# Banded attention of a streaming encoder layer: each split float32r product triple against one plain float32 product

## Chip, cores and metric

The kernel runs on one core of a Trainium2 chip. The metric is device microseconds (us) from start to end. TensorE (PE) multiplies, VectorE (DVE), ScalarE (ACT) and GpSimd (POOL) do the rest, and DMA queues move data between HBM and SBUF. A difference of about 0.2% (3.3 us) is the least that a measurement of this kernel tells from no change.

## What is computed

One layer of a chunk-causal streaming encoder on 1024 prompt tokens and 64 sample tokens, in float32. The part in question is the banded attention of the mixer: 8 heads of 64, chunks of 64 tokens, each chunk attending to itself and the 8 chunks before it.

```python
def chunk_band_attention(qc, kb, vb, key_valid, rel_bias, offset):
    ...
    s = jnp.einsum('bnqhd,bnkhd->bnhqk', qc, kb).astype(jnp.float32) * (HEAD_DIM_B ** -0.5) + bias[None, None]
    s = jnp.where(key_valid[None, :, None, None, :], s, NEG)
    p = jax.nn.softmax(s, axis=-1).astype(vb.dtype)
    return jnp.einsum('bnhqk,bnkhd->bnqhd', p, vb)
```

Before it come an input projection, two convolution mixers and the RMS norms of q and k; after it an output projection, cross attention and an MLP.

## The kernel before

Activations lie transposed, features on the partitions and 1092 token columns along the free axis. The large projections run through `pe_part` (L444), which multiplies a value split into a high and a low float32r part as high·high + high·low + low·high. The banded attention is written in the same way.

It is done for four head pairs j = 0..3, one after another, and each pair in nine units b = 0..8 of 128 queries (36 units n = 9j + b). Unit b has min(b+1, 5) key blocks of 128 (the last one, the sample tokens, reads 512 cached keys and 64 new ones). The two heads of a pair lie on partitions 0 to 63 and 64 to 127.

A unit passes through these steps:

- `scores(n)` on PE (L2397): for each head, three products q_hi·k_hi, q_lo·k_hi, q_hi·k_lo into PSUM banks 0 to 2.
- `biased(n)` on DVE (L1804): adds the bias tile of the pair and takes the row minimum, once per head. It waits for `bias_ready`, two memsets on POOL (L895, L897) that follow the DMA of the bias tile.
- `exps(n)` on ACT (L1229): exponential with the row sum, in place in `scores`.
- `transposes(n)` on PE (L2461): 128x128 transposes of the exponentials, up to ten, into banks 4 to 6, in up to three pieces of two key blocks.
- `pt_hi(n)` on ACT (L1247) copies each piece to float32r, and `pt_lo(n)` on DVE (L1827) forms the rest.
- `values(n)` on PE (L2483): three products per key block, 128x256, into bank 7; `o_out(n)` on ACT (L1238) copies the result out.

PE runs the cycle of unit n in program order: `transposes(n)`, an item a, `values(n-1)`, `scores(n+2)`, an item b. The items are small jobs for the next head pair: x = 0..2 and 3..5 broadcast the RMS factors of q and k through PE (L2390) for a multiplication on DVE (L1764), x = 6..8 transpose the v columns (L2383) for a copy, and x = 9..11 divide the output by the sums. After the first pair all items use PSUM bank 3, so PE starts an item only when the consumer of the last one has read that bank. DVE runs the cycle as the piece copies of unit n, item a, `biased(n+2)`, item b. Each engine takes its instructions strictly in this written order.

For pair 0 the nine items and the high and low parts of q, k and v are made before `scores(0)`. For the later pairs ACT makes the high parts (`q_hi`, `k_hi`, `v_hi`, `cache_hi`), DVE the low part of v and POOL those of q, k and the cache (L423, L429).

Of the kernel before, what the change touches and what calls it, by code (L numbers as in the profile page):

```python
# [13 lines left out]
P = 128  # L14
# [36 lines left out]
class Semaphores:  # L51

    def __init__(self, sem):
# [78 lines left out]
        self.qk2_hi = sem("qk2_hi")  # L132
        self.qk2_lo = sem("qk2_lo")
        self.kc_hi = sem("kc_hi")
        self.kc_lo = sem("kc_lo")
        self.v_hi = sem("v_hi")
        self.v_lo = sem("v_lo")
# [7 lines left out]
        self.pt_hi = sem("pt_hi")  # L145
        self.pt_lo = sem("pt_lo")
# [73 lines left out]
class BandOperands:  # L220

    def __init__(self, Q, K, V, KC, VC):
        self.Q, self.K, self.V, self.KC, self.VC = Q, K, V, KC, VC

# [5 lines left out]
def build(nc, xT, memT, slabs, wdn, params, rbrev, ctxa, ctxc, kcT, vc, mkcT, mvc,  # L230
          o_y, o_ca, o_cc, o_k, o_v, o_kc, o_vc, o_mk, o_mv):
    ctx = ExitStack()
    with ctx:
# [55 lines left out]
        QKV = [slot(f"q_raw{j}", 12 + j) for j in range(4)] + [slot(f"k_raw{j}", 8 + j) for j in range(4)] \  # L289
# [5 lines left out]
        for r in range(2):  # L295
            o = A0 + 8 * r * TB
            AT.append(BandOperands(
                Q=[at(f"q_hi{r}", [P, T], F32R, o), at(f"q_lo{r}", [P, T], F32R, o + TB)],
                K=[at(f"k_hi{r}", [P, T], F32R, o + 2 * TB), at(f"k_lo{r}", [P, T], F32R, o + 3 * TB)],
                V=[at(f"v_hi{r}", [P, 9, P], F32R, o + 4 * TB), at(f"v_lo{r}", [P, 9, P], F32R, o + 4 * TB + 4608)],  # L300
                KC=[at(f"kc_hi{r}", [P, 512], F32R, o + 4 * TB + 9216),
                    at(f"kc_lo{r}", [P, 512], F32R, o + 4 * TB + 11264)],
                VC=[at(f"vc_hi{r}", [P, 4, P], F32R, o + 4 * TB + 13312),
                    at(f"vc_lo{r}", [P, 4, P], F32R, o + 4 * TB + 15360)]))
# [3 lines left out]
        PT = [[at(f"pt_{n}{r}", [P, 4, 256], F32R, W0 + 4096 * (2 * r + x)) for x, n in enumerate(("hi", "lo"))]  # L308
              for r in range(2)]
        PT5 = [[at("pt5_hi0", [P, 256], F32R, W0 + 16384), at("pt5_lo0", [P, 256], F32R, W0 + 17408)],  # L310
               [at("pt5_hi1", [P, 256], F32R, W0 + 23552), at("pt5_lo1", [P, 256], F32R, B0 + 15360)]]
# [4 lines left out]
        RKC = at("kc_raw", [P, 512], F32, R0 + 4608)  # L316
        RVC = at("vc_raw", [P, 4, P], F32, R0 + 6656)
# [98 lines left out]

        def cache_lo(e, j):

            r = AT[j % 2]
# [127 lines left out]
        for n in range(N_U):  # L547
            CUM.append(CUM[-1] + pieces(n))

# [2250 lines left out]
```

## Time and profile before

| | |
|---|---|
| median of 3 runs | 1665.53 us (1664.52 to 1666.72) |
| profiled execution | 1665.04 us |
| its span (first to last instruction) | 1663.3 us |
| mean granted TensorE clock | 0.981 of full speed |
| PE / DVE / ACT / POOL busy | 95% / 59% / 40% / 18% |
| chain that ended last | PE 82%, DVE 5%, ACT 4%, DMA 4%, issue 3% |

The span and the profiled execution's time differ by 1.7 us of start and end around the instructions. The chain is the sequence of work that ended last, followed back through what each step waited for. A mean over the program hides that the attention stage has other limits than the projections around it, so that stage has to be read alone.

### The profile page before, as it was taken

The numbers are of one execution on the slowest core, as the hardware profiler recorded it, in microseconds if no ns is written. First come the engines' busy times: TensorE is split into PE (matmuls) and PEld (weight loads), VectorE is DVE, ScalarE is ACT, GpSimd is POOL, SyncE is SP. The second block draws the span as 40 slices with busy tenths as digits, with TensorE's granted clock in tenths as the row PEclk, the third lists the DMA queues.
The fourth block names the chain that finished last, engine by engine and source line by source line (L and its number), as shares of the span: only waits on it lengthen the run. The fifth ranks groups of instructions, "written<-read, shape, count | busy, mean of one in ns | idle before, by whom it ended". The sixth has DMA issues, their size and how long they took to land.

```text
span 1663.3 us, 27523 instructions
## 1 busy us (share of the span) xinstructions
PE 1580.0 (95%) x11220; PEld 1545.5 (93%) x11220; DVE 980.6 (59%) x1393; ACT 658.1 (40%) x1154; POOL 305.3 (18%) x354
## 2 busy tenths in 40 slices
PE   6999999997889999997789999999999899999999
PEld 6999999995788899997679999999999899999999
DVE  6626776536778644245653477666666558646653
ACT  5521021136889532124531363333333333333332
POOL 1011000002220010002410005444455411010110
PEclk9999999988999999999989999999999999999999
DMA  7425111002110153101051215333333686354563
GB/s 245 143 91 171 40 39 39 26 1 93 37 37 34 51 174 134 48 14 51 26 184 54 92 40 184 146 146 145 146 145 147 234 288 220 96 168 147 159 211 110
DMA packets 63666, 189.37 MB, mean 114 GB/s; under 512 B 7872, under 2 KB 13048, under 8 KB 63408
## 3 DMA queue, kind: packets, MB, share of 16 engines
q1 hardware_dynamic: 37904, 91.11, 16.6%
q0 software_dynamic: 25648, 96.65, 16.1%
q8 instruction: 83, 1.36, 0.3%
q14 instruction: 31, 0.25, 0.1%
HBM read 138.58 MB, written 54.12 MB: 116 GB/s over the span
## 4 chain that ended last, share of the span: by engine, by line
PE 82%; DVE 5%; ACT 4%; DMA 4%; issue 3%; POOL 1%; SPq 0%; ACTq 0%; DVEq 0%; POOLq 0%
PE ps L454 33%; PE ps L2707 18%; PE ps L2728 17%; PE ps L2235 3%; PE ps L483 2%; PE ps L2483 2%; DMA a<-wdn 2%; PE ps L2606 2%; PE ps L2423 1%; PE ps L2461 1%; DVE scores L1804 1%; ACT scores L1229 1%; DVE t_raw L2084 1%; PE ps L505 1%; PE ps L2390 1%
## 5 line engine op out<-in xcount | busy, mean ns | idle before, releaser
L454 PE MATMUL ps<-A_hi,w_hi 128*128 128x364 f32 x768 | 173.6, 335 | 0.0
L454 PE MATMUL ps<-A_hi,w_lo 128*128 128x364 f32 x768 | 170.0, 329 | 0.0
L454 PE MATMUL ps<-A_lo,w_hi 128*128 128x364 f32 x768 | 169.9, 329 | 0.0
L395 DVE TENSOR_TENSOR w_lo<-w_raw,w_hi 128x1024 fp32r<-128x1024 f32 x43 | 52.5, 1223 | 151.6 <-ACT w_hi L391 151.2
L391 ACT ACTIVATE w_hi<-w_raw 128x1024 fp32r<-128x1024 f32 x42 | 44.3, 1057 | 241.5 <-PE ps L454 136.3
L454 PEld LDWEIGHTS ps<-A_lo,w_hi 128*128 128x128 f32 x768 | 134.4, 189 | 0.0
L454 PEld LDWEIGHTS ps<-A_hi,w_lo 128*128 128x128 f32 x768 | 134.0, 189 | 0.0
L454 PEld LDWEIGHTS ps<-A_hi,w_hi 128*128 128x128 f32 x768 | 133.7, 190 | 0.0
L2707 PE MATMUL ps<-t_hi,wq_hi 128*128 128x272 f32 x480 | 100.9, 292 | 7.2 <-DVE hid_stage L2130 4.3
L2707 PE MATMUL ps<-t_lo,wq_hi 128*128 128x272 f32 x480 | 100.5, 291 | 0.0
L2707 PE MATMUL ps<-t_hi,wq_lo 128*128 128x272 f32 x480 | 100.1, 290 | 0.0
L2728 PE MATMUL ps<-r_hi_a,wq_hi 128*128 128x272 f32 x448 | 93.3, 290 | 3.1 <-DVE r_lo_a L2170 3.1
L2728 PE MATMUL ps<-r_lo_b,wq_hi 128*128 128x272 f32 x448 | 93.5, 290 | 0.0
L2728 PE MATMUL ps<-r_hi_b,wq_lo 128*128 128x272 f32 x448 | 93.3, 289 | 0.0
L2728 PE MATMUL ps<-r_hi_b,wq_hi 128*128 128x272 f32 x448 | 93.3, 289 | 0.0
L2728 PE MATMUL ps<-r_lo_a,wq_hi 128*128 128x272 f32 x448 | 93.1, 289 | 0.0
L2728 PE MATMUL ps<-r_hi_a,wq_lo 128*128 128x272 f32 x448 | 93.0, 289 | 0.0
L2707 PEld LDWEIGHTS ps<-t_hi,wq_hi 128*128 128x128 f32 x480 | 76.3, 191 | 7.8 <-issue 7.8
L2707 PEld LDWEIGHTS ps<-t_lo,wq_hi 128*128 128x128 f32 x480 | 76.7, 192 | 0.0
L2707 PEld LDWEIGHTS ps<-t_hi,wq_lo 128*128 128x128 f32 x480 | 76.4, 191 | 0.0
L1655 DVE SCALAR_TENSOR_TENSOR conv_acc<-ua_ext,params,conv_acc 128x1118 f32<-128x1118 f32 x58 | 76.1, 1375 | 0.0
L2707 PE MATMUL ps<-A_hi,wq_lo 128*128 128x272 f32 x360 | 74.5, 288 | 0.0
(342 smaller groups left out, 4095.1 us busy)
## 6 DMA issues: line engine op xcount, KB each, us to landing
w_raw<-slabs SPq DMA_DIRECT2D x68, 512.0 KB, 3.4
quads_d<-quad_sum POOLq DMA_DIRECT2D x64, 272.0 KB, 3.2
w_raw<-wdn POOLq DMA_DIRECT2D x32, 512.0 KB, 4.1
r_raw_a<-quads_d SPq DMA_DIRECT2D x56, 272.0 KB, 2.9
r_raw_b<-quads_d SPq DMA_DIRECT2D x56, 272.0 KB, 2.9
quads_d<-hid_stage POOLq DMA_DIRECT2D x48, 272.0 KB, 2.8
Y<-xT POOLq DMA_DIRECT2D x16, 546.0 KB, 4.7
y_d<-Y POOLq DMA_DIRECT2D x16, 546.0 KB, 3.1
```

What stands on the lines that cost most here:

```text
L391: e.activation(WH[:, par], RAW[:, par], ACT.Copy).then_inc(s.w_hi, 1)
L395: e.tensor_tensor(WL[:, par], RAW[:, par], WH[:, par].bitcast(F32), ALU.subtract).then_inc(s.w_lo, 1)
L454: ins = e.matmul(PS[:, 3 * par + c, 0:CH], wt[:, wpar, w], xt[:, col:col + CH], start=(first and n == 0 and m == 0), stop=(last and n == l ...
L483: ins = e.matmul(PS[:, 6, 2 * b:2 * b + 2], src[:, t0:t0 + P], rhs[:, :], start=(n == 0), stop=(n == len(pairs) - 1))
L505: ins = e.transpose(PS[:, bank, BLK[b] - lo:BLK[b] - lo + P], src(b), ID[:, :])
L1229: e.activation(SS[n % 2][:, h, 0:cols], SS[n % 2][:, h, 0:cols], ACT.Exp, bias=MIN[:, m:m + 1], scale=-1.0, accum_out=ESUM[:, n, h:h + 1]) ...
L1655: e.scalar_tensor_tensor(CAV[:, h], UE[:, h, j:j + CAW], w, CAV[:, h], ALU.mult, ALU.add)\
L2235: ins = e.matmul(PS[:, 3 * par, 0:NMEM], wt[:, par, k * P:(k + 1) * P], xt[:, k * NMEM:(k + 1) * NMEM], start=(k == 0 and m == 0), stop=(k ...
L2483: ins = e.matmul(PS[:, 7, 0:256], lhs, rhs, start=(kt == 0 and m == 0), stop=(kt == tiles - 1 and m == 2))
L2606: ins = e.matmul(PS[:, 6 + d, 0:w], r.KV[vx][:, vv, v0:v0 + P], XPT[px][:, k, 0:w], start=(n == 0), stop=(n == 5))
L2707: ins = e.matmul(PS[:, b + c, 0:HC], WQ[wx][:, q % 4, k * P:(k + 1) * P], right(i, xx, k, c), start=(i in (0, 1, 3) and k == 0 and m == 0) ...
L2728: ins = e.matmul(PS[:, 2 * g + c, 0:HC], WQ[wx][:, down_slot(n), g * P:(g + 1) * P], down_right(xx, n)[:, c * HC:(c + 1) * HC], start=(ii ...
```

## The change

Each split product of the banded attention becomes one product of plain float32 operands. The high and low parts, and all instructions that made them, are gone: `q_hi`, `k_hi`, `cache_hi`, `v_hi` on ACT, `qk_lo` and `cache_lo` on DVE and POOL. `scores` reads `q_raw` and `k_raw` directly, with the order of its parts changed, and waits for q and k in thirds and not for the whole. The cache goes by DMA straight into its operand tiles. The v blocks are copied once, on DVE (`v_copy`). Of the transposed exponentials ACT copies piece 0 and DVE pieces 1 and 2, each once (`pt_copy`). For pair 0 the items run in the order 0, 3, 1, 2, 4 to 8, with `scores(0)` and `biased(0)` after the second of them and `scores(1)` and `biased(1)` after the fourth. The q and k tiles of the pairs lie in other slots.

```diff
-            def pt_hi(n):
-                for p in range(pieces(n)):
-                    rows, w = piece(n, p)
-                    e.wait_ge(s.t_done, CUM[n] + p + 1)
-                    if n >= 2:
-                        e.wait_ge(s.pv_done, n - 1)
-                        e.wait_ge(s.pt_lo, CUM[n - 1])
-                    e.activation(pt_piece(0, n, p), PS[0:rows, 4 + p, 0:w], ACT.Copy).then_inc(s.pt_hi, 1)
+            def pt_copy(n):
+                rows, w = piece(n, 0)
+                e.wait_ge(s.t_done, CUM[n] + 1)
+                if n >= 2:
+                    e.wait_ge(s.pv_done, n - 1)
+                e.activation(pt_piece(n, 0), PS[0:rows, 4, 0:w], ACT.Copy).then_inc(s.pt_act, 1)
...
-            def pt_lo(n):
-                for p in range(pieces(n)):
+            def pt_copy(n):
+                for p in range(1, pieces(n)):
                     rows, w = piece(n, p)
-                    e.wait_ge(s.pt_hi, CUM[n] + p + 1)
-                    e.tensor_tensor(pt_piece(1, n, p), PS[0:rows, 4 + p, 0:w], pt_piece(0, n, p).bitcast(F32),
-                                    ALU.subtract).then_inc(s.pt_lo, 1)
+                    e.wait_ge(s.t_done, CUM[n] + p + 1)
+                    if n >= 2:
+                        e.wait_ge(s.pv_done, n - 1)
+                    e.tensor_copy(pt_piece(n, p), PS[0:rows, 4 + p, 0:w]).then_inc(s.pt_dve, 1)
...
-            for x in range(9):
+            e.wait_ge(s.ya_done, 2)
+            for n, x in enumerate(FIRST_ITEMS):
                 item(0, x)
-                if x in (5, 8):
-                    qk_lo(e, 0, (x - 5) // 3)
-            e.wait_ge(s.ya_done, 2)
-            biased(0)
-            biased(1)
+                if n in (1, 3):
+                    biased(n // 2)
...
                 if tail <= 0:
-                    for m in range(3):
-                        ins = [part(h, m, M[h]) for h in range(2)]
-                    ins[0].then_inc(s.s_done, 1)
-                    ins[1].then_inc(s.s_done, 1)
+                    for h in range(2):
+                        part(h, M[h]).then_inc(s.s_done, 1)
                     return
...
+                part(1, M[1])
                 if b == 8:
-                    for m in range(3):
-                        part(1, m, (r.K, SEQ, 64, 512))
-                e.wait_ge(s.s_done, 2 * n + 1)
-                for m in range(3):
-                    ins = part(1, m, X[1])
-                ins.then_inc(s.s_done, 1)
+                    part(1, (K, SEQ, 64, 512))
+                part(0, X[0]).then_inc(s.s_done, 1)
+                part(0, M[0]).then_inc(s.s_done, 1)
+                e.wait_ge(s.s_done, S_CUM[n] + 1)
+                part(1, X[1]).then_inc(s.s_done, 1)
...
-                    for m, (vx, px) in enumerate(((0, 0), (0, 1), (1, 0))):
-                        if b < 8:
-                            lhs = r.V[vx][:, max(0, b - 4) + kt]
-                        else:
-                            lhs = r.VC[vx][:, kt] if kt < 4 else r.V[vx][0:w, 8]
-                        rhs = PT[n % 2][px][0:w, kt] if kt < 4 else PT5[n % 2][px][0:w, :]
-                        ins = e.matmul(PS[:, 7, 0:256], lhs, rhs,
-                                       start=(kt == 0 and m == 0), stop=(kt == tiles - 1 and m == 2))
+                    if b < 8:
+                        lhs = r.V[:, max(0, b - 4) + kt]
+                    else:
+                        lhs = r.VC[:, kt] if kt < 4 else r.V[0:w, 8]
+                    rhs = PT[n % 2][0:w, kt] if kt < 4 else PT5[n % 2][0:w, :]
+                    ins = e.matmul(PS[:, 7, 0:256], lhs, rhs, start=(kt == 0), stop=(kt == tiles - 1))
```

On PE, the scores of a unit with five key blocks (128x512 is the main part of one head, 128x128 its tail) were these before:

```order
L2423 MATMUL ps<-k_hi_104,q_hi_102 128x128 [waits ttr_done]
L2423 MATMUL ps<-k_hi_104,q_hi_102 128x512
L2423 MATMUL ps<-k_hi_104,q_lo_103 128x128
L2423 MATMUL ps<-k_lo_105,q_hi_102 128x128
L2423 MATMUL ps<-k_hi_104,q_hi_102 128x512
L2423 MATMUL ps<-k_hi_104,q_lo_103 128x512 x2
L2423 MATMUL ps<-k_lo_105,q_hi_102 128x512 x2
L2423 MATMUL ps<-k_hi_104,q_hi_102 128x128 [waits s_done]
```

In the change the same place, with the values of the unit before it (L2400), reads:

```order
L2400 MATMUL ps<-pt_112,v_102 128x256 [waits pt_act,o_used]
L2400 MATMUL ps<-pt_112,v_102 128x256
L2400 MATMUL ps<-pt_112,v_102 128x256 [waits pt_dve]
L2400 MATMUL ps<-pt_112,v_102 128x256
L2400 MATMUL ps<-pt_114,v_102 128x256 [waits pt_dve]
L2347 MATMUL ps<-k_raw_89,q_raw_85 128x512 [waits ttr_done]
L2347 MATMUL ps<-k_raw_89,q_raw_85 128x128
L2347 MATMUL ps<-k_raw_89,q_raw_85 128x512
L2347 MATMUL ps<-k_raw_89,q_raw_85 128x128 [waits s_done]
```

Twelve score products became four, and fifteen value products five. The parts of the two heads alternated product by product; now each head's part stands as one instruction.

On DVE, at the start of pair 0, these rows stood before (neg_max rows belong to the bias step):

```order
L1764 SCALAR_TENSOR_TENSOR k_raw_89<-k_raw_89,params,ps 128x384 [waits bc_done] x2
L1764 SCALAR_TENSOR_TENSOR k_raw_89<-k_raw_89,params,ps 128x324 [waits bc_done]
L429 TENSOR_TENSOR q_lo_103<-q_raw_85,q_hi_102 128x1092 [waits qk2_hi]
L1772 TENSOR_TENSOR v_lo_107<-ps,v_hi_106 128x384 [waits v_hi] x2
L1772 TENSOR_TENSOR v_lo_107<-ps,v_hi_106 128x256 [waits v_hi]
L1775 TENSOR_TENSOR v_lo_107<-ps,v_hi_106 64x128
L429 TENSOR_TENSOR k_lo_105<-k_raw_89,k_hi_104 128x1092 [waits qk2_hi]
L1804 ISA scores_122,neg_max<-ps,bias_124 128x128 [waits s_done,bias_ready,ya_done]
```

And these stand there now:

```order
L1690 SCALAR_TENSOR_TENSOR q_raw_85<-q_raw_85,gq_scaled,ps 128x384 [waits bc_done,ya_done,gq_ready]
L1690 SCALAR_TENSOR_TENSOR k_raw_89<-k_raw_89,params,ps 128x384 [waits bc_done]
L1731 ISA scores_108,neg_max<-ps,bias_110 128x128 [waits s_done,bias_ready]
L1731 ISA neg_max 128x1
L1731 ISA scores_108,neg_max<-ps,bias_110 128x128
L1731 ISA neg_max 128x1
L1690 SCALAR_TENSOR_TENSOR q_raw_85<-q_raw_85,gq_scaled,ps 128x384 [waits bc_done]
L1690 SCALAR_TENSOR_TENSOR q_raw_85<-q_raw_85,gq_scaled,ps 128x324 [waits bc_done]
L1731 ISA scores_109,neg_max<-ps,bias_110 128x256 [waits s_done,bias_ready]
```

The first bias step, with its wait for `bias_ready`, moved ahead of seven of the nine items of pair 0.

## Rows read from the trace of the kernel before

**Rows 1.** Work by stage: us, then busy us (and count) of PE, weight loads, DVE, ACT, POOL, then granted clock, DMA share, GB/s.

```profile
385.00:560.00 175.00, 152.09 (x1215) 134.72 (x1214) 127.19 (x301) 147.29 (x357) 32.66 (x33) 0.95 0.13 45
```

**Rows 2.** Chain that ended last, in order of time: start us, length us, what.

```profile
461.40 1.09 PE ps L2461 x10
...
473.27 0.37 PE ps L2461 x2
...
514.26 0.37 PE ps L2461 x2
...
553.71 0.48 PE ps L2390 x3
...
560.19 1.90 PE ps L483 x18
```

**Rows 3.** PE's first transposes of each unit, timeline: start us, us, engine, line, operation, xcount.

```profile
392.45 0.69 PE L2461 MATMUL ps<-ident,scores 128*128 128x128 f32 x2
...
433.97 0.44 PE L2461 MATMUL ps<-ident,scores 128*128 128x128 f32 x2
...
439.67 0.82 PE L2461 MATMUL ps<-ident,scores 128*128 128x128 f32 x6
444.90 1.04 PE L2461 MATMUL ps<-ident,scores 128*128 128x128 f32 x8
450.01 1.26 PE L2461 MATMUL ps<-ident,scores 128*128 128x128 f32 x10
455.42 1.25 PE L2461 MATMUL ps<-ident,scores 128*128 128x128 f32 x10
461.24 1.25 PE L2461 MATMUL ps<-ident,scores 128*128 128x128 f32 x10
465.59 1.31 PE L2461 MATMUL ps<-ident,scores 128*128 128x128 f32 x10
```

**Rows 4.** Timeline of one cycle with two items: [idle before <-releaser] at the end.

```profile
452.47 0.28 PE L2483 MATMUL ps<-pt_lo,v_hi 128*128 128x256 f32 x1
...
453.61 0.28 PE L2483 MATMUL ps<-pt_hi,v_lo 128*128 128x256 f32 x1
453.81 0.50 PE L2423 MATMUL ps<-k_hi,q_hi 64*128 64x128 f32 x2
...
455.03 0.55 PE L2390 MATMUL ps<-ident,rstd_heads 128*128 128x128 f32 x3
455.26 0.82 DVE L1804 CUSTOM_DVE_ANT_0 scores<-ps,bias 128x640 f32<-128x640 f32 x1 [1.30 <-issue]
...
457.42 0.55 PE L2390 MATMUL ps<-ident,rstd_heads 128*128 128x128 f32 x3 [0.75 <-DVE k_raw L1764]
```

**Rows 5.** Timeline, scores of a unit with 512 keys: six products.

```profile
438.16 0.50 PE L2423 MATMUL ps<-k_hi,q_hi 64*128 64x512 f32 x2
...
438.73 0.39 PE L2423 MATMUL ps<-k_lo,q_hi 64*128 64x512 f32 x2
```

**Rows 6.** Plain float32 products (line 483): duration ns min/median/max, first and last start.

```profile
L483 PE MATMUL ps<-half_sel,square x144: 166/251/251, 235.2 to 338.8; 128*128 128x2 f32 x144
```

**Rows 7.** Groups of the stage 385 to 553: busy us, mean ns, idle before with its releasers.

```profile
L1827 DVE TENSOR_TENSOR pt_lo<-ps,pt_hi 128x512 fp32r<-128x512 f32 (+2 forms) x84 | 45.6, 589 | 6.2 <-ACT pt_hi L1247 5.6
L1247 ACT ACTIVATE pt_hi<-ps 128x512 fp32r<-128x512 f32 (+2 forms) x84 | 38.9, 526 | 8.1 <-PE ps L2461 7.5
```

**Rows 8.** Timeline at the start of pair 0, POOL and DVE.

```profile
379.95 1.81 DVE L1764 SCALAR_TENSOR_TENSOR q_raw<-q_raw,gq_scaled,ps 128x384 f32<-128x384 f32 x3
...
388.99 0.20 POOL L897 MEMSET bias<- 64x128 f32 x1
...
390.94 0.29 DVE L1804 CUSTOM_DVE_ANT_0 scores<-ps,bias 128x128 f32<-128x128 f32 x1 [1.23 <-PE ps L2423]
```

**Rows 9.** Work by stretch, columns as in rows 1.

```profile
394.00:398.00 4.00, 4.00 (x19) 2.64 (x17) 1.75 (x6) 3.61 (x12) 0.00 (x0) 0.50 0.00 0
...
482.00:486.00 4.00, 4.00 (x25) 3.59 (x25) 1.25 (x3) 2.55 (x8) 1.43 (x2) 0.60 0.00 0
```

More of the change, by code:

```diff
@@ L288, in build @@
         CAV = at("conv_acc", [P, 2, CAW], F32, B0 + 9216)
-        QKV = [slot(f"q_raw{j}", 12 + j) for j in range(4)] + [slot(f"k_raw{j}", 8 + j) for j in range(4)] \
+        QKV = [slot(f"q_raw{j}", (14, 8, 10, 12)[j]) for j in range(4)] \
+            + [slot(f"k_raw{j}", (15, 9, 11, 13)[j]) for j in range(4)] \
             + [slot(f"v_raw{j}", 7 - j) for j in range(4)]
@@ L297, in build @@
             AT.append(BandOperands(
[L298 to L304, printed above, removed]
+                V=at(f"v{r}", [P, 9, P], F32, o + 4 * TB),
+                KC=at(f"kc{r}", [P, 512], F32, o + 4 * TB + 9216),
+                VC=at(f"vc{r}", [P, 4, P], F32, o + 4 * TB + 13312)))
         SS = [at(f"scores{r}", [P, 2, 640], F32, B0 + 5120 * r) for r in range(2)]
         BIAS = [at("bias0", [P, 2, 640], F32, B0 + 10240), at("bias1", [P, 2, 640], F32, W0 + 18432)]
[L308 to L311, printed above, removed]
+        PT = [at(f"pt{r}", [P, 4, 256], F32, W0 + 5120 * r) for r in range(2)]
+        PT5 = [at(f"pt5{r}", [P, 256], F32, W0 + 5120 * r + 4096) for r in range(2)]
         RX = at("rstd_heads", [P, 9, 2, 64], F32, R0)
@@ L600, in score_cols @@
             return PS[:, 0:3].rearrange("p a b -> p (a b)")[:, c0:c0 + cols], c0
+        S_CUM = [0]
+        for n in range(N_U):
+            S_CUM.append(S_CUM[-1] + (3 if n % 9 >= 4 else 2))
         RXN = {(0, 0): 1, (0, 1): 2}
@@ L1268, in _ @@
             rstd_heads(0, 1)
-            q_hi(0)
-            k_hi(0)
-            for c in range(3):
-                v_hi(0, c)
             exps(0)
             for n in range(N_U):
-                pt_hi(n)
+                pt_copy(n)
                 if n + 1 < N_U:
@@ L1857, in ya_norm @@
                 ins.then_inc(s.bc_used, 1)
-            for x in range(9):
+            e.wait_ge(s.ya_done, 2)
+            for n, x in enumerate(FIRST_ITEMS):
                 item(0, x)
-                if x in (5, 8):
-                    qk_lo(e, 0, (x - 5) // 3)
-            e.wait_ge(s.ya_done, 2)
-            biased(0)
-            biased(1)
+                if n in (1, 3):
+                    biased(n // 2)
             for n in range(N_U):
@@ L2450, in transposes @@
                 for p in range(pieces(n)):
-                    if n:
-                        e.wait_ge(s.pt_lo, CUM[n - 1] + min(p + 1, pieces(n - 1)))
+                    if n and p == 0:
+                        e.wait_ge(s.pt_act, n)
+                    elif n and CUM_D[n]:
+                        e.wait_ge(s.pt_dve, CUM_D[n - 1] + min(p, pieces(n - 1) - 1))
                     if p == 2 and last[6]:
```

164 lines of the change are left out of this document (50 added, 114 removed).

## Prediction

> **What bounds the kernel now.** I read the clock first (0.981, one core, nothing to compare), then the work by stage. In the attention stage PE is busy for 152 of 175 us and ACT for 147 [rows 1]; the projections before and after it do not change. So the question is what the end of the attention does, when item (3,11) on PE (553.71, 0.48 us long [rows 2]) lets the first out-projection product start. Everything behind it waits for PE and should move as one block.
>
> The chain of waits runs from pair 0 to the middle of pair 3 mostly over PE's own instructions. The starts of the transposes give the period of each unit. In pair 1 they are 433.97, 439.67 (b = 2), 444.90, 450.01, 455.42, 461.24, 465.59 [rows 3], and 473.27 for the next pair [rows 2]. As periods: 5.70 for b = 0 and 1 together, then 5.23, 5.11, 5.41, 5.82, 4.35, and 7.68 for b = 7 and 8, which is 39.3 us for the pair. Pair 0 takes 41.5 (392.45 to 433.97 [rows 3]), pair 2 takes 41.0 (473.27 to 514.26), pair 3 takes 39.5 (514.26 to 553.71 [rows 2]).
>
> One cycle shows why. PE ends the scores at 455.03; DVE needs until 457.42 (two bias steps of about 0.82 and an item) before PE may start the next item, and PE stands idle for 0.75 of these 2.39 us [rows 4]. The rest is PE at work. So a pair is PE work plus about 4 us of such stalls, in cycles b = 2 to 5. ACT's and DVE's work counts only through those stalls and in pair 3, where ACT also squares and splits for the next stage.
>
> **The price of a plain product.** The trace has none with a wide moving operand, so I bound it. The statistic products of line 483 are plain float32 with 2 columns. The program has 8 times 9 of those with half_sel, and the trace shows x144 [rows 6]: a plain product is recorded as two passes. Eighteen records take 1.90 us [rows 2], 0.106 us each, for 2 columns: the floor of a pass. Ten float32 transposes take 1.09 us [rows 2], 0.109 each for 128 columns in one pass. So a pass costs at most about 0.107 per 128 columns, if a product streams as a transpose does. A float32r value product takes (453.61 - 452.47)/10 = 0.114 for 256 columns [rows 4].
>
> Low end: a plain pass streams as fast as float32r, 256 columns in 0.114, so a value product is 0.23. High end: 0.214 per pass, 0.43 per product. I take the high end: the operand is plain float32, and the row nearest in operand type is the transpose. At 0.43 one plain product costs more than the three split ones, 0.34.
>
> The Trainium skill (FP8 and Floating Point Precision, TensorE Precision Notes) says that true float32 takes four passes through the array. No run here shows it for a wide product. By it a value product would cost four times 0.107, the same 0.43.
>
> **Values.** 140 key blocks: 140 x 0.43 = 60 us against 140 x 0.34 = 48. That adds 12 us.
>
> **Scores.** The heads use different halves of the rows, and their products run side by side: two pairs of 512-column products start within 0.57 us (438.16 to 438.73 [rows 5]), 0.29 per pair where one alone streams for 0.21 to 0.23. Of a five-block unit the twelve products take 455.03 - 453.81 = 1.22 us [rows 4]. In the change a 512-column pass lasts 0.43, and each head's two passes follow each other. If the next head's first pass starts beside the last head's second, a five-block unit takes 7/2 of such passes, 1.5 us; if nothing overlaps, 5 x 0.43 = 2.13. For b = 0 to 3: 0.43, 0.64, 0.96, 1.28 with overlap and up to 0.43, 0.85, 1.28, 1.71 without. For b = 8: 1.6 to 2.2 against 1.3.
>
> **What is removed.** ACT loses 48 of 84 piece copies of 0.526, and DVE 36 of 84 of 0.589 [rows 7], besides all q, k, v and cache splits. In cycles b = 2 to 5 of pairs 0 to 2 this buys little: the stall there is the bias steps and the item, which stay. I let the stall end 2.0 us after the transposes start (2.39 less the item b of 0.33 on PE); for b = 2, whose v copy no longer goes ACT then DVE, 1.75.
>
> **New periods**, T for transposes at 0.107 each, item 0.33:
> - b = 0: T 0.2 + values 2.13 + scores 0.96 to 1.28 = 3.3 to 3.6. b = 1: 0.43 + 0.33 + 0.43 + 1.28 to 1.71 + 0.33 = 2.8 to 3.2. Together 6.1 to 6.8 against 5.70.
> - b = 2: 1.75 + 0.33 + values 0.85 + 1.5 to 2.13 + 0.33 = 4.8 to 5.4 against 5.23.
> - b = 3, 4, 5: 2.0 + 0.33 + values 1.28, 1.71, 2.13 + scores + 0.33 = 5.5, 5.9, 6.3 to 6.1, 6.5, 6.9 against 5.11, 5.41, 5.82.
> - b = 6: 1.07 + 2.13 + 1.6 to 2.2 = 4.8 to 5.4 against 4.35. b = 7 and 8: each T 1.07 + item 0.33 + values 2.13, and the scores 0.43 and 0.64 to 0.85 of the next pair's first units: 8.1 to 8.3 against 7.68.
>
> Sum 41.5 to 45.4 us: pair 1 gets 2.2 to 6.1 us longer, and pair 2, which before took 1.7 us more (at 482 to 486 PE was granted 0.60 of its clock [rows 9]), 0.5 to 4.4.
>
> **Pair 3.** No items b. ACT's extra squares hold b = 1 and 2 as before, less one copy: about 0.4 us back. The last units have no scores left. Period by period I get 37.6 to 40.5 against 39.5: -1.9 to +1.0.
>
> **The start of pair 0.** DVE does one q item of about 0.6 at 379.95 (three took 1.81 [rows 8]) and one k item behind it, so `scores(0)` can run at about 382. But the first bias step waits for the memset that ends at 389.19, only 1.75 us ahead of where it started before (390.94) [rows 8]; the DMA ahead of it keeps its place. DVE stands still from about 382, for some 7 us, and seven items are queued behind: the transposes of unit 0 come after item 8 on PE. From 389.2: bias 0.5, two items 1.2, a wait for scores(1) 0.4, bias 0.85, two items 1.2, first v copy and its wait 0.8, last v transposes 0.9: about 395.1 against 392.45, so +2.6. Hidden before, by work that DVE did while the bias tile was on its way. PE is nearly idle till then. It had the lower of its two levels, 0.50 (1.2 GHz), in 394 to 398 [rows 9], and will have it again, with passes twice as long in units 0 to 2: +0.6. From there pair 0 follows the periods above, less the wait for the cache DMA that ACT had: +0.5 to +3.7. Pair 0 in all: +3.7 to +6.9.
>
> **Sum.** 4.5 to 18.4 us: pair 0 3.7 to 6.9, pair 1 2.2 to 6.1, pair 2 0.5 to 4.4, pair 3 -1.9 to 1.0. I believe in overlap of the heads, since float32r shows it, so I stay in the lower half; small per-pass floors come on top. I take +10.5. The profiled execution is 1665.04 and the median 1665.53, so 1676.
>
> **Rivals.**
> - *No overlap between the heads' plain passes.* For it: each head's passes now stand together. Against it: rows 5. The high ends of all sums: +18, 1684. Chance 0.2.
> - *Fast plain passes* (the other side): 256 columns in 0.114. The place is every values and scores step: five-block units need 1.14 for values and 0.86 for scores (8 passes of 0.107), so periods b = 2 to 5 fall to 3.7 to 4.7 and the others to 2.3 to 3.6. A pair takes about 32.5, 7 us less in pairs 1 and 2; pairs 0 and 3 gain 8 together: -22, 1643. It decides once a 256-column product costs less than about 0.34. For it: no row excludes it, since transposes may be held by their weight loads. Against it: the operand type. Chance 0.09.
> - *Weight loads not hidden.* A plain pass would pay its stream and its load of 0.106 in turn. 280 value passes give +30 and the scores about +15 over my sum: 1720. Against it: float32r hides the load (256 columns in 0.114). The Trainium skill (TensorE: Matmul & The Clock Gate, Part 3) says that weight loads overlap running products only where the row group differs. By that rule both passes of a product would pay; the trace disagrees for float32r, and no row shows plain. Chance 0.05.
> - *The stalls shrink.* If DVE, relieved, lets items go 0.7 us earlier in twelve cycles, 8 us come back: about 1667, no change. Against it: bias steps and item alone fill the 2.39 us. Chance 0.11.
>
> **How the numbers follow.** My case (1671 to 1680) has 0.55. The range reaches to no overlap above and to the vanished stalls below: 1665 to 1688. A difference of 0.2% is about what a measurement tells. Slower: my case, no overlap and unhidden loads, 0.80, less 0.03 for a sum that lands near zero: 0.77. Same: the shrunk stalls and that 0.03, less a little: 0.12. Faster: 0.11.
>
> **What would show it.** PE's value records: two per product, starts 0.21 apart. Scores of a five-block unit: 1.5 us. Transposes of unit 0 at 395, those of pair 1 at 438 to 441; pair 1 some 42 to 44 us long; an idle DVE from 382 to 389; ACT busy far less with no gain. The prediction is wrong if value records start 0.11 apart, or if the idle PE time in cycles b = 2 to 5 disappears.

## The result, and the profile after

| | before | changed kernel |
|---|---|---|
| median | 1666.22 us (1660.99 to 1672.52, 16 runs) | 1669.99 us (1665.79 to 1679.33, 16 runs) |
| profiled execution, span | 1665.04, 1663.3 us | 1670.03, 1668.2 us |
| mean granted clock | 0.981 | 0.982 |

The ratio is 1.0033 with an interval of 1.002 to 1.0047: the change costs 3.3 to 7.8 us. The forecast was 1676 with a range of 1665 to 1688, and slower at 0.77. The direction and the range held. The size did less well: 1.0033 is 5.5 us, about half of the +10.5 that was taken.

The busy times of the whole program, on the page of the changed kernel, have moved as if the change were harmless: ACT falls from 40% to 37% and DVE from 59% to 58%, while PE goes from 95% to 96%.

```profile
PE 1595.2 (96%) x10964; PEld 1534.9 (92%) x10964; DVE 960.6 (58%) x1353; ACT 622.7 (37%) x1074; POOL 283.4 (17%) x342
...
PE 84%; DVE 5%; DMA 4%; ACT 3%; issue 3%; POOL 1%; SPq 0%; DVEq 0%; ACTq 0%; POOLq 0%
```

The chain of waits dates the pairs: the first transposes of pairs 1, 2 and 3, a five-block set of values, and item (3,11), the answers to [rows 2].

```profile
437.00 0.37 PE ps L2377 x2
...
467.92 2.16 PE ps L2400 x10
...
480.21 0.37 PE ps L2377 x2
...
523.42 0.37 PE ps L2377 x2
...
563.52 0.48 PE ps L2314 x3
```

Pair 1 lasts 480.21 - 437.00 = 43.2 us (39.3 before), pair 2 lasts 43.2 (41.0), pair 3 lasts 40.1 (39.5).

To compare executions I measure the stage from a mark at which both kernels have done the same work: from the start of DVE's last `v_raw` instruction of the projection to item (3,11). The two marks in front, before and after the change:

```profile
377.48 1.29 DVE L1594 TENSOR_TENSOR v_raw<-ps,rstd 128x1092 f32<-128x1092 f32 x1 [2.07 <-PE ps L454]
```

```profile
378.75 1.29 DVE L1520 TENSOR_TENSOR v_raw<-ps,rstd 128x1092 f32<-128x1092 f32 x1 [2.70 <-PE ps L428]
```

The stage was 553.71 - 377.48 = 176.2 us and is 563.52 - 378.75 = 184.8: 8.5 us more. The work between these marks, before and after (columns as in [rows 1]; the window of [rows 1] itself reaches 6 us into the next projection before the change and ends inside the stage after it):

```profile
377.48:553.71 176.23, 151.28 (x1216) 132.65 (x1216) 129.32 (x310) 147.71 (x357) 36.79 (x40) 0.95 0.14 47
```

```profile
378.75:563.52 184.77, 166.52 (x960) 121.73 (x960) 105.69 (x270) 112.14 (x276) 14.09 (x28) 0.96 0.14 45
```

PE has 256 instructions fewer and yet 15 us more to do; ACT has 36 us less, DVE 24 us less, POOL 23 us less. The stage still got longer.

The spans differ by only 4.9, so outside the stage this execution of the changed kernel was 3.6 us shorter, in code that did not change. That is why the stage, and not the total, is the measure below.

The cycle of [rows 4], at the same place in the changed kernel (unit b = 4 of pair 1):

```profile
453.93 1.25 PE L2377 MATMUL ps<-ident,scores 128*128 128x128 f32 x10
455.85 0.55 PE L2314 MATMUL ps<-ident,rstd_heads 128*128 128x128 f32 x3 [0.67 <-DVE v L1700]
456.23 1.89 PE L2400 MATMUL ps<-pt,v 128*128 128x256 f32 x8
458.05 1.68 PE L2347 MATMUL ps<-k_raw,q_raw 64*128 64x512 f32 x8
459.67 0.55 PE L2314 MATMUL ps<-ident,rstd_heads 128*128 128x128 f32 x3
460.05 1.25 PE L2377 MATMUL ps<-ident,scores 128*128 128x128 f32 x10
```

Read it by starts: transposes and stall 1.92 us, item 0.38, values 1.82 for four key blocks, scores 1.62, item 0.38. The cycle is 6.12 us. PE's idle time ahead of the item is 0.67 us, where [rows 4] had 0.75 (the cycle ahead of this one has 0.94): the stall stayed here, though the pieces are now copied once and by two engines in parallel. From the start of the transposes to the item, the cycles b = 3, 4 and 5 of pair 1 took 2.00, 1.95 and 2.00 us before and take 1.98, 1.92 and 1.98; only b = 2, where PE waits for DVE's part in the copy of v, fell, from 2.45 to 1.66. And there are eight value records for four products: each plain product is recorded as two passes.

The start of pair 0 (POOL and DVE, the answer to [rows 8]):

```profile
381.25 0.61 DVE L1690 SCALAR_TENSOR_TENSOR q_raw<-q_raw,gq_scaled,ps 128x384 f32<-128x384 f32 x1
383.03 0.61 DVE L1690 SCALAR_TENSOR_TENSOR k_raw<-k_raw,params,ps 128x384 f32<-128x384 f32 x1 [1.17 <-PE ps L2314]
390.18 0.20 POOL L875 MEMSET bias<- 64x128 f32 x1
390.42 0.29 DVE L1731 CUSTOM_DVE_ANT_0 scores<-ps,bias 128x128 f32<-128x128 f32 x1 [6.78 <-POOL bias L875]
```

DVE stands still for 6.78 us for the bias tile, with seven items queued behind that wait. The first transposes then come at 395.78.

### The profile page after: what moved, and what is told of

It reads as the page before. It is cut to its first block, busy times and chain, and to the rows that moved or that the text cites. A ratio compares the mean times of both kernels' runs of the same rounds, so it can differ in the third digit from the quotient of the medians.

```text
span 1668.2 us, 26883 instructions
## 1 busy us (share of the span) xinstructions
PE 1595.2 (96%) x10964; PEld 1534.9 (92%) x10964; DVE 960.6 (58%) x1353; ACT 622.7 (37%) x1074; POOL 283.4 (17%) x342
## 4 chain that ended last, share of the span: by engine, by line
PE 84%; DVE 5%; DMA 4%; ACT 3%; issue 3%; POOL 1%; SPq 0%; DVEq 0%; ACTq 0%; POOLq 0%
PE ps L428 33%; PE ps L2623 17%; PE ps L2644 17%; PE ps L2400 3%; PE ps L2159 3%; PE ps L457 2%; DMA a<-wdn 2%; PE ps L2347 2%; PE ps L2522 2%; PE ps L2377 1%; DVE scores L1731 1%; DVE t_raw L2008 1%; PE ps L2490 1%; PE ps L2314 1%; PE ps L479 1%
## 5 line engine op out<-in xcount | busy, mean ns | idle before, releaser
L1731 DVE CUSTOM_DVE_ANT_0 scores<-ps,bias 128x640 f32<-128x640 f32 (+5 forms) x72 | 45.4, 667 | 71.8 <-issue 51.3
```

The costliest lines, as they stand in the source:

```text
L1731: e.tensor_tensor_reduce(out=SS[n % 2][:, h, 0:cols], in0=score_cols(n, h)[0], in1=BIAS[j % 2][:, h, off:off + cols], scale=1.0, scalar=3e ...
```

## The experiments

All stage lengths are by the marks named above. One table first, and the readings after it. Each ratio is to runs of the kernel before on the same chip, whose medians were 1663.31 to 1666.22 us.

| kernel | what it is | median, us | ratio to before | stage, us | pairs 0 to 3, us |
|---|---|---|---|---|---|
| before | | 1666.22 | | 176.2 | 41.5, 39.3, 41.0, 39.5 |
| changed | | 1669.99 | 1.002 to 1.0047 | 184.8 | 41.2, 43.2, 43.2, 40.1 |
| e10_after_again | changed, again | 1671.69 | 1.0035 to 1.0078 | 184.8 | 41.2, 43.2, 43.2, 40.1 |
| e11_before_again | before, again | one run | | 176.2 | 41.7, 39.2, 40.9, 39.3 |
| e1_bias_first | changed, bias tile sooner | 1666.59 | 0.9985 to 1.0022 | 179.3 | 41.2, 43.2, 43.2, 40.1 |
| e6_before_bias_first | before, bias tile sooner | 1663.75 | 0.9979 to 1.0016 | 174.5 | 40.5, 39.2, 39.3, 39.4 |
| e2_item_first | changed, item b first | 1665.27 | 0.9991 to 1.0025 | 177.6 | 38.8, 40.8, 40.8, 40.1 |
| e4_before_item_first | before, item b first | 1673.50 | 1.0027 to 1.0061 | 184.4 | 45.9, 41.5, 41.5, 39.4 |
| e8_before_qk_first | before, only q and k items first | 1664.13 | 0.9983 to 1.0014 | 173.8 | 41.3, 38.2, 39.8, 39.5 |
| e5_values_r | changed, values in float32r | 1642.89, one run | | 153.2 | 32.2, 34.3, 34.3, 35.4 |
| e9_score_order_only | changed, head 0's tail first | 1666.25 | 0.999 to 1.0039 | 179.2 | 39.7, 41.7, 41.7, 38.8 |
| e3_both | e1 and e2 | 1662.52 | 0.9956 to 0.9998 | 171.5 | 38.8, 40.8, 40.8, 40.1 |
| e7_score_order | e3 and the order of e9 | 1652.62 | 0.9916 to 0.9959 | 166.2 | 37.2, 39.3, 39.3, 38.8 |

### The same kernels again

First, how well a stage length repeats. Neither kernel is edited.

> The changed kernel unchanged, profiled again. Its first profile shows the stage, from the last v_raw row to item (3,11), 8.6 us longer than before, but the measured total only 3.3 to 7.8 us longer. Theory (the stage is the same in each execution, and the stretches outside vary by some us): the stage comes out at 184.7 again within 0.5 us and the total anywhere in the known spread. Rival (the first profile was a slow one in this stage): below 183.

> The kernel before unchanged, profiled again. Its first profile had PE at 0.60 of its clock in 482 to 486, inside the stage. Theory (this drop comes and goes with the execution): the stage comes out between 174 and 176.2, with pair 2 near 39.3 or 41 us. Rival (the drop belongs to the kernel): pair 2 again at 41 us and the stage at 176.2.

The changed kernel gave the same 184.8 us, and each of its 36 periods to within 0.01 or 0.02 us. The kernel before gave 176.2 again, with single periods up to 0.07 us apart, and with the slow cycle b = 2 of pair 2 in it (6.75 us, against 5.21 in pair 1). The windows of [rows 9] in e11_before_again:

```profile
394.00:398.00 4.00, 4.00 (x19) 3.04 (x19) 2.15 (x6) 3.63 (x11) 0.00 (x0) 0.50 0.00 0
482.00:486.00 4.00, 4.00 (x23) 3.61 (x24) 1.30 (x3) 3.09 (x8) 0.86 (x1) 0.57 0.00 0
```

My expectation that the lower clock in pair 2 comes and goes by chance fell: it came again in the same cycle. Two executions have pair 2's extra 1.5 us there. The changed kernel doesn't have it, neither in units 0 and 1 of pair 0 (395.78 to 399.85) nor in pair 2:

```profile
396.00:400.00 4.00, 3.79 (x21) 1.80 (x20) 1.93 (x7) 3.28 (x11) 1.25 (x2) 1.00 0.92 282
482.00:486.00 4.00, 3.98 (x21) 2.03 (x19) 1.44 (x5) 2.35 (x10) 2.00 (x3) 1.00 0.37 99
```

In both windows of before PE was busy for all 4.00 us and granted half or little more, that is its level of 1.2 GHz for most of the stretch; after, it had all of its 2.4 GHz. The other split kernels have such stretches too, in other places. First e6_before_bias_first in pair 3, then e4_before_item_first twice in pair 0:

```profile
525.50:528.50 3.00, 3.00 (x15) 2.86 (x13) 3.00 (x6) 2.98 (x6) 0.00 (x0) 0.50 0.00 0
```

```profile
411.00:414.00 3.00, 3.00 (x16) 3.00 (x16) 1.53 (x4) 1.66 (x4) 0.00 (x0) 0.50 0.63 209
425.00:427.00 2.00, 2.00 (x12) 2.00 (x11) 1.86 (x6) 1.45 (x4) 0.76 (x1) 0.50 0.00 0
```

So all five profiles of split kernels have a stretch at the lower level inside the attention, beyond the one at the start of pair 0. None of the eight profiles of plain kernels has one: their granted clock is 1.00 over 400 to 560. Part of what the splits save is lost to the clock, and the 8.5 us are net of that. What takes the clock down in those cycles I haven't found.

### The wait for the bias tile

Theory: the 6.78 us idle of DVE come from where the tile's DMA stands in POOL's queue, behind the v output stores and the cache loads, more than from the tile's own journey. The edit issues pair 0's tile ahead of those (e6 does the same to the kernel before); in e1 a wait for the last cache load also goes ahead of each later one, which no period shows. The main part of the edit (`load_bias(0)` then only sets the mask):

```diff
+            g.wait_ge(s.rep_out, 16)
+            g.wait_ge(s.ya_done, 2)
+            g.wait_ge(s.w_lo, S_OUT)
+            g.wait_ge(s.tile_done, S_OUT)
+            g.dma_start(BIAS[0][:, :, :], bass.AP(rep_d.tensor, 127,
+                                                          [[8 * 768 - 1, P], [768, 2], [1, 640]])).then_inc(s.bias_in, 16)
             g.wait_ge(s.tile_read, S_IN + 22)
             for j in range(4):
...
```

> The changed kernel with one move: on POOL the DMA of pair 0's bias tile is issued ahead of the four o_v stores and the two cache loads, where its source and its target are free. Theory (the start is held by the bias tile): in the changed kernel the mask ends at 390.4 and the transposes of unit 0 start at 395.8, 17.0 us after the last v_raw row starts. The tile should now be ready near 385, and unit 0's transposes should start 11 to 12 us after that row, so 5 to 6 us less in all, about the time of the kernel before. Rival (the nine items on PE and DVE hold the start, not the bias tile): unit 0 starts less than 2 us earlier and the total gains under 2 us. Second rival (given back later by the half clock or the next DMA): unit 0 is early, but the units 0 to 8 take longer by as much.

> The kernel before, with the DMA of pair 0's bias tile issued ahead of the o_v stores and the cache loads on POOL. It is the counterpart of the same move in the changed kernel. Theory (before, DVE's splits cover the time in which the tile is on its way): unit 0's transposes start 15 us after the last v_raw row as before, the stage keeps its 176 us within 1 us, and the time does not move. Rival (the tile was already late before): the stage shrinks by 2 us or more.

Timeline of e1_bias_first, POOL and DVE:

```profile
382.45 0.72 POOL L896 DMA_DIRECT2D bias<-bias_rep_d  x1 [186.66 <-PE ps L428]
...
387.84 0.20 POOL L880 MEMSET bias<- 64x128 f32 x1
388.07 0.29 DVE L1744 CUSTOM_DVE_ANT_0 scores<-ps,bias 128x128 f32<-128x128 f32 x1 [1.32 <-POOL bias L880]
```

DVE now waits 1.32 us for the tile and not 6.78. In e1 the transposes of unit 0 come 11.59 us after `v_raw`, not 17.03, and no period after that changes: the stage gives back exactly those 5.4 us. The tile is issued 0.59 us after `v_raw` and not 5.01 us, and the way from issue to memset took 5.1 us where it took 6.2.

In the kernel before the same edit brings nothing for the start: PE's first scores wait for DVE's `k_lo` there, since DVE has the nine items and the splits to do while the tile is on its way. e6's start is 16.03 us and not 14.97, which I had not expected, but that isn't the edit's doing: e4, whose start of pair 0 is not edited, has 16.03 too. In both PE was granted 0.50 over the 6 us from 3 us after `v_raw`, where in before it was granted 1.00 over 380 to 386. e6's stage is 1.7 us shorter all the same, more than the 1 us I had allowed: its pair 2 runs without the slow cycle (5.20 us in place of 6.76), pair 0 is 1.0 us shorter, and its own stretch of lower clock in pair 3 leaves that pair's length as it was.

So the bias wait was covered before, and the reordering of the items laid it bare. That time was lost in this wait is shown. The price of the new start is the net of the wait laid bare, the copies that were saved and the clock: 17.03 - 14.97 = 2.06 us against before, 1.0 us against the start of e4 and e6.

### Item b ahead of the scores

Theory: in cycles b = 2 to 5 PE waits for DVE, since item a needs bank 3, which the last item's consumer frees only behind two bias steps. If item b goes ahead of the scores on PE and ahead of the bias step on DVE, the bank is free in time.

```diff
                 if n:
                     values(n - 1)
+                for j, x in items_b(n):
+                    item(j, x)
                 if n + 2 < N_U:
                     scores(n + 2)
-                for j, x in items_b(n):
-                    item(j, x)
```

This is PE's part. DVE has the same exchange with `biased(n + 2)`. e4 makes it in the kernel before, e8 there for q and k items alone (`if x < 6`).

> The changed kernel with item b of each cycle ahead of scores(n+2) on PE and ahead of biased(n+2) on DVE, nothing else. Theory (a pair is PE work plus the stall of PE for the item that DVE reads only behind two bias steps): DVE now does item b while PE makes the scores, so the idle times of 0.67 to 0.94 us before the items of b = 2 to 5 go, and pairs 1 and 2 shrink from 43.2 to 39.5 to 40.5 us; the total gains 8 to 11 us over the changed kernel and ends 3 to 5 us below the kernel before. Rival (DVE or ACT holds the cycle): the stall reappears at the transposes or at the scores, and the pairs stay above 42 us.

> The kernel before (split products) with item b ahead of scores(n+2) and biased(n+2). It asks whether split products profit from the same order. Theory (PE work decides once the stall is gone): the split form has 12 us less of value products and gains the same stalls, 8 to 10 us, so near 1657, and stays below the changed kernel with that order by 4 to 8 us. Rival (without the stalls the split form is held by ACT and DVE, which copy each piece twice): it gains less than 5 us, and the plain form with the same order is level or faster.

> The kernel before, with item b ahead of the scores and the bias step only where it is a q or k item; v items stay behind. With all items ahead the split form got 8 us slower, and DVE's v_lo waited 22.7 us for ACT's v_hi. Theory (the split v item has to pass through ACT, which is in the exponentials, and holds DVE's bias step): with the v items back in place the stage is below that of the kernel before, by the 0.96 and 0.75 us stalls behind the q and k items in each of three pairs, so 4 to 5 us, near 171. Rival (ACT holds the split form in any order): the stage stays within 1 us of 176.

PE's timeline of e2_item_first in pair 1, b = 3 to 5:

```profile
450.55 1.31 PE L2377 MATMUL ps<-ident,scores 128*128 128x128 f32 x10
...
455.93 1.31 PE L2377 MATMUL ps<-ident,scores 128*128 128x128 f32 x10
...
457.40 2.32 PE L2400 MATMUL ps<-pt,v 128*128 128x256 f32 x10
...
461.60 1.31 PE L2377 MATMUL ps<-ident,scores 128*128 128x128 f32 x10
```

No row of that stretch has an idle time in brackets any more. The periods b = 2 to 5 fall from 5.00, 5.75, 6.12, 6.61 to 4.55, 4.99, 5.38, 5.67, which is 2.9 us a pair, and b = 1 grows by 0.4. The 2.9 us are nearly the 3.2 us that PE stood idle ahead of the items of pair 1 (0.85, 0.94, 0.67, 0.73). Pairs 1 and 2 come to 40.8 us, just outside the 39.5 to 40.5 I expected, and the stage is 7.2 us shorter, a little under the 8 to 11. The total ends level with the kernel before (0.9991 to 1.0025) and not 3 to 5 us below it. What is left in those periods is PE's own work: transposes, values, scores and items.

The surprise is e4. In the kernel before I took the exchange to be harmless or a gain; the stage got 8.2 us longer. Pair 1, which ran at full clock in both, gives the clean price: it takes 41.5 us, where before, e11 and e6 have 39.2 to 39.3, so 2.3 us a pair. In the sum, 1.1 us is the later start of pair 0 that e6 has as well, and pair 0 (45.9 us) holds the two stretches at half clock shown above, while pair 2 has none. DVE's waits, first of before and then of e4_before_item_first (us in total, times, longest):

```profile
DVE v_lo L1772 <- ACT v_hi L1196: 3.2, 4, 1.0
DVE v_lo L1772 <- ACT v_hi L1199: 1.1, 1, 1.1
```

```profile
DVE v_lo L1772 <- ACT v_hi L1196: 14.3, 7, 2.7
...
DVE v_lo L1772 <- ACT v_hi L1199: 8.4, 4, 3.4
```

A v item there is a chain: PE transposes, ACT forms the high part, DVE the low part. Moved ahead of the bias step, it makes DVE wait for ACT with both bias steps queued behind it: 22.7 us of waiting in place of 4.3. e8, which moves only the items without that chain, turns the loss into a gain of 2.4 us of stage, under the 4 to 5 I expected, since cycles b = 2 and b = 4 got 0.4 and 0.5 us longer. Without the v items the moves bring pair 1 to 38.2 us, with them to 41.5, so the v items are what made e4 slow. In the plain form v is copied once, by one engine, and there the exchange of all items gains. That the single engine is what makes the difference there is argued, since no run copies v over two engines in the plain form.

### The price of a plain value product

The value products of the units b < 8 read the same data as float32r, one product and no low part. That leaves the low parts of v and of the exponentials out of the computation. All else is the changed kernel's.

```diff
-                V=at(f"v{r}", [P, 9, P], F32, o + 4 * TB),
+                V=at(f"v{r}", [P, 9, P], F32R, o + 4 * TB),
...
-        PT = [at(f"pt{r}", [P, 4, 256], F32, W0 + 5120 * r) for r in range(2)]
-        PT5 = [at(f"pt5{r}", [P, 256], F32, W0 + 5120 * r + 4096) for r in range(2)]
+        PT = [at(f"pt{r}", [P, 4, 256], F32R, W0 + 5120 * r) for r in range(2)]
+        PT5 = [at(f"pt5{r}", [P, 256], F32R, W0 + 5120 * r + 4096) for r in range(2)]
...
```

> The changed kernel with the value products of b = 0 to 7 as one float32r product each; the tiles of v and of the transposed exponentials are float32r, and the low parts are left out, so the values are less exact than float32. b = 8 stays plain. Theory (PE's plain passes set the period wherever no stall does): the records of a value product start 0.11 apart, one per product, and periods shrink by 0.32 us per key block: b = 6 and 7 (whose values are those of the five-block units before) by 1.6 at most, from 4.97 and 4.15 to about 3.5, where ACT's and DVE's own work for a unit holds them; the stage loses 30 to 38 us. Rival (the plain form is held by ACT, DVE or the buffers): periods shrink by less than half of that.

Groups of the stage in e5_values_r (busy us, mean ns of one): 120 products of the units b < 8 as one record each, and those of b = 8 still plain, two records each.

```profile
L2402 PE MATMUL ps<-pt,v 128*128 128x256 f32 x120 | 21.9, 302 | 0.0
L2402 PE MATMUL ps<-pt,vc 128*128 128x256 f32 x32 | 7.7, 383 | 0.7 <-ACT Y L1172 0.7
```

The stage falls by 31.6 us, within the 30 to 38 expected. Periods b = 6 and 7, where PE has nothing to wait for, give the price: 4.97 to 3.40 and 4.15 to 2.58, 1.57 us for five products, 0.31 each. I had expected ACT's and DVE's own work to hold both near 3.5, but b = 7 went on to 2.58. Periods b = 2 to 5 of pair 1 shrink by 0.62, 0.95, 1.25 and 1.58, the same 0.31 for each of their two to five blocks. A plain product at 0.43 less one in float32r at 0.114 is 0.32. The rival that plain passes stream as fast as float32r ones is gone, and so is the one that some other wait would hold the cycles at their length once the values were cheap.

### The order of the score products

The two heads use different halves of PE's rows, and the records show a plain product of one head run beside one of the other. In the changed kernel a five-block unit issues head 1's main part, head 0's tail, head 0's main part, head 1's tail. The edit puts head 0's tail first, alone in e9, and on top of e3 in e7:

```diff
+                part(0, X[0]).then_inc(s.s_done, 1)
                 part(1, M[1])
                 if b == 8:
                     part(1, (K, SEQ, 64, 512))
-                part(0, X[0]).then_inc(s.s_done, 1)
                 part(0, M[0]).then_inc(s.s_done, 1)
```

> The changed kernel with only the order of the score parts changed: the tail of head 0 goes ahead of the main part of head 1. Theory (the last product waits for a signal that stands behind head 1's main part): it saves 0.28 us in each unit of five key blocks, 20 of them, 5 to 6 us in all, also without the other two moves: stage near 179, total about level with the kernel before. Rival (the saving in the kernel with all three moves came from their interplay): the stalls for the items take it back and the stage stays above 182.

> Both moves of the two kernels ahead of it in one. Theory: the start and the stalls are separate, so the gains add: 13 to 16 us below the changed kernel, near 1656. Rival (they share their cover): clearly less than the sum.

> The changed kernel with both moves (bias tile early, item b ahead), and in scores the tail of head 0 issued ahead of the main part of head 1. There, the last product of head 1 waits for the tail's semaphore, and it starts only 1.20 us after the first product, at the end of head 0's second pass, though the tail streamed at 0.01 to 0.3. Theory (signals come in program order, so the tail's signal stands behind head 1's main part): now the signal comes early, the last product runs beside head 0's second pass, the scores of a five-block unit take 1.3 to 1.4 us and not 1.62, and the stage loses 4 to 6 us to about 166, the total near 1657. Rival (the array takes the passes one head at a time at the end): scores stay at 1.6 and nothing moves.

e9 takes 5.6 us off the stage, and 0.28 to 0.33 us off each period in which a five-block unit's scores are issued (5.75, 6.12, 6.61 to 5.45, 5.83, 6.32 for b = 3 to 5; 4.97 to 4.69 for b = 6). In the records of the changed kernel the last tail of head 1 ran alone at the end: its two passes started 1.20 and 1.41 us into the group, behind head 0's main part, and the group ended at 1.62. With head 0's tail first, head 1's tail no longer runs alone: its passes start at 0.97 and 1.08, beside the end of head 0's main part. The group takes 439.27 - 437.99 = 1.28 in e7_score_order's timeline.

```profile
437.99 1.35 PE L2360 MATMUL ps<-k_raw,q_raw 64*128 64x128 f32 x8
439.27 1.09 PE L2390 MATMUL ps<-ident,scores 128*128 128x128 f32 x8
```

e3 and e7 show that the three gains add: 5.4 + 7.2 = 12.6 against 13.3 measured for e3, and 5.3 more for e7. The pairs of e3 are those of e2 to 0.02 us; the 0.7 beyond the sum is its start, 10.99 us after `v_raw` where e1 and e7 have 11.59. e3's total, though, is 1662.52 and not near the 1656 expected. e7's work between its marks, and its chain:

```profile
379.57:545.80 166.23, 159.62 (x960) 122.26 (x960) 106.66 (x270) 111.73 (x276) 14.04 (x28) 0.98 0.15 50
```

```profile
467.72 0.37 PE ps L2390 x2
...
545.80 0.48 PE ps L2327 x3
```

PE is busy for 96% of the stage, against 90% in the changed kernel. e7 is the fastest of those that leave no low part out: 1652.62 us, 0.9916 to 0.9959 of the kernel before, with plain products throughout. Whether plain products are better than split ones is another question. The kernel before was only given the other item order and the sooner bias tile, one at a time, and never another order of its score products. The best split kernel stays untested.

## Why the prediction was right, and where a term was off

**Direction and size.** Term by term, forecast against measured:

| term | forecast, us | measured, us |
|---|---|---|
| start of pair 0 | +2.6 | 17.03 - 14.97 = +2.1 |
| units 0 and 1 of pair 0 | half clock again, +0.6, and a part of +0.5 to +3.7 | 4.1 against 6.3, -2.2 |
| rest of pair 0 | the rest of +0.5 to +3.7 | +1.9 |
| pair 1 | +2.2 to +6.1 | +3.9 |
| pair 2 | +0.5 to +4.4 | +2.2 |
| pair 3 | -1.9 to +1.0 | +0.6 |
| stage | 4.5 to 18.4, taken 10.5 | +8.5 |

**The term that was mis-sized** is pair 0. The text says of its first units that PE "had the lower of its two levels, 0.50 (1.2 GHz), in 394 to 398 [rows 9], and will have it again, with passes twice as long in units 0 to 2: +0.6", and gives pair 0 +3.7 to +6.9 in all. It measured +1.8: +2.1 at the start, -2.2 in units 0 and 1, +1.9 behind them. The step that failed is the clock: PE did not have the lower level again in these units. It had 1.00 over 396 to 400, as the window above shows, and before it had 0.50 from 390 to 398. Before, the transposes of units 0 to 2 started as in the first fence; after, as in the second:

```profile
392.45 0.69 PE L2461 MATMUL ps<-ident,scores 128*128 128x128 f32 x2
394.79 1.12 PE L2461 MATMUL ps<-ident,scores 128*128 128x128 f32 x4
398.75 1.36 PE L2461 MATMUL ps<-ident,scores 128*128 128x128 f32 x6
```

```profile
395.78 0.38 PE L2377 MATMUL ps<-ident,scores 128*128 128x128 f32 x2
397.21 0.84 PE L2377 MATMUL ps<-ident,scores 128*128 128x128 f32 x4 [0.21 <-ACT scores L1163]
399.85 0.82 PE L2377 MATMUL ps<-ident,scores 128*128 128x128 f32 x6
```

Two transposes that took 0.69 us took 0.38. In unit 1 before, from 394.79 to 398.75, PE was busy without a pause (4.00 of 4.00 us from 394 to 398), so its 3.96 us are PE's work at half clock; after, with costlier products, it took 2.64. In unit 0 PE also waited before (0.39 us for DVE), and copies and splits between the first units had gone too. How unit 0's 0.9 us divide between clock and copies no run separates.

The clock helped in pair 2 as well. The text had counted it there: 0.5 to 4.4 for pair 2 is the term of pair 1 less 1.7.

**The price of a plain product** was right: 0.214 per pass from the transposes, and ten value records in 2.16 us are 0.216 each (the x10 row of the chain above). The forecast had to choose between two rows, the float32r product with 256 columns and the float32 transpose. It chose by the type of the operand, and e5 measures the difference directly. The 12 us for the 140 products were a little too much, since the split ones cost more than 0.34 each. The values of unit b = 4 of pair 1, up to the scores behind them, before and after:

```profile
457.72 0.37 PE L2483 MATMUL ps<-pt_hi,v_hi 128*128 128x256 f32 x1
...
459.62 0.50 PE L2423 MATMUL ps<-k_hi,q_hi 64*128 64x128 f32 x2
```

```profile
462.41 2.32 PE L2400 MATMUL ps<-pt,v 128*128 128x256 f32 x10
464.66 0.69 PE L2347 MATMUL ps<-k_raw,q_raw 64*128 64x512 f32 x2
```

Five key blocks went from 1.90 to 2.25 us, 0.07 each and not 0.09: about 10 us over 140 blocks. In pair 1, by starts, values took 2.1 us more, scores 2.0 more, items 0.6 more, and the transposes with the stalls behind them 0.7 less. That is its +3.9.

**Overlap of the heads.** It was right that plain passes of the two heads run side by side, and the sizes were off both ways. For 512 keys the text priced 1.28 us; the row is 1.06:

```profile
441.74 1.13 PE L2347 MATMUL ps<-k_raw,q_raw 64*128 64x512 f32 x4
442.80 0.55 PE L2307 MATMUL ps<-ident,v_raw 128*128 128x128 f32 x3
```

The four 512-column passes start in two couples, near 441.74 and near 442.25, so both heads run beside each other throughout, at about 0.5 us for a couple; I had let only the middle two of the four overlap (three times 0.43). For five blocks the text priced 1.5 and the unit took 1.62, for the lone tail that e9 and e7 removed. These errors nearly cancel over a pair: the nine score steps were priced at 10.9 us in all and measure 11.0. That is luck: one error hides the other.

**Stalls.** The end of the stall, put at 2.0 us after the transposes start, measured 1.92 (453.93 to 455.85). The rival in which DVE, relieved, lets items go sooner fell: DVE and ACT together lost 59 us of work between the marks, and the idle time ahead of an item of this cycle went from 0.75 to 0.67. In the whole stage PE's idle time ahead of the items of L2390 and L2314 fell from 12.4 to 8.7 us. In pairs 1 and 2 that is cycle b = 2 almost alone, whose stall the text let end at 1.75 and which measured 1.66. e2 shows what takes the rest: another order, not less work.

**Weight loads.** They are hidden behind plain passes. 240 loads for the values take 190 ns each and the passes still start 216 ns apart; unhidden, a pass would cost its stream and its load.

```profile
L2400 PEld LDWEIGHTS ps<-pt,v 128*128 128x128 f32 x240 | 43.1, 190 | 4.5
```

Nearly all value passes use all 128 rows, so by the rule of the Trainium skill (TensorE: Matmul & The Clock Gate, Part 3), that loads overlap products only where the row group differs, each would have paid. This trace disagrees with it for plain operands too. It agrees with another sentence of the same section, which the prediction left out: that PE also pulls a load ahead when it goes to the background weight buffer. Whether these loads went there no run shows.

**Start of pair 0.** The idle DVE, its cause and the items queued behind it were as told: 6.78 us against "some 7". The transposes of unit 0 came at 395.78 where the text has 395, in an execution that reached the stage 1.3 us later.

**What stays open.** The stage says +8.5 us, the ratio of the first comparison 3.3 to 7.8, that of the second 5.8 to 13.0. The code outside the stage is the same, and its time varies by several us between executions: from item (3,11) to the end 1106.0 to 1112.1 us in the five profiles of split kernels, and 1103.5 to 1111.0 in the eight of plain ones. The ranges overlap, so whether the changed kernel really gains some us there, these runs can't tell. The forecast of 10.5 us was for the whole program. It was near the stage and far from the 5.5 us of the first ratio, and what lies between the two is not explained.

## What to carry to other kernels

One plain float32 product on all rows costs more than three float32r ones of the same shape (0.43 us against 0.34 to 0.38 for 256 columns), so removing splits pays only where the engines that make the splits are what PE waits for; here they mostly weren't, and 82 us less work on ACT, DVE and POOL in the stage (36, 24 and 23) did not shorten it until the order was changed. For scores on half the rows the two forms are nearly level: 0.96 us split [rows 5] and 1.06 plain for 512 keys, 1.22 split and 1.28 plain for five blocks in the order of e7. Before moving an instruction ahead, list what is queued behind its waits: the same exchange of an item and a bias step gained 2.4 us a pair with a one-engine copy and cost 2.3 us a pair with a two-engine chain. A wait that looks free, as that for the bias tile did, is free only as long as the work in front of it stays in front.

## What the runs showed of the hardware

- Products that read different halves of the rows overlap almost fully when both are plain float32: four passes of 512 columns took 1.06 us. Estimated from the 0.216 that 256 columns take, four in a row would need 1.73 and two couples side by side 0.86. The product left without a partner makes a group longer, so the order of the parts alone was worth some 0.3 us per unit.
- A lower granted clock can belong to one cycle of one kernel: 0.60 and 0.57 in the same 4 us of two executions, and e8 has it in that cycle too (6.80 us) with yet another order. Pair 1 passed the same code without it. In e6 and e4, where the clock fell sooner at the start of pair 0, it is not in pair 2 but in pair 3 and pair 0. All five split profiles have such a stretch inside the attention, none of the eight plain ones has. I know no cause.
- PE's stretches repeated to 0.02 us between executions of the changed kernel, over 36 periods, and to 0.07 us in the kernel before. The several us by which executions of one kernel differ come from the stages around this one.
